# One VectorE-summed mean-square product in place of eight, in a hybrid decoder step on one Trainium2 core

## The reference, cut to what matters

```
def rmsnorm(x, w):
    x32 = x.astype(jnp.float32)
    y = x32 * lax.rsqrt(jnp.mean(x32 * x32, axis=-1, keepdims=True) + RMS_EPS)
    return (y * w.astype(jnp.float32)).astype(x.dtype)
...
    def sub_in(t, i):
        return rmsnorm(t, norm_pre[i]) * (1.0 + m_scale[:, i, None]) + m_shift[:, i, None]

    def sub_out(t, y, i, res):
        return t + res * m_gate[:, i, None] * rmsnorm(y, norm_post[i])

    x = sub_out(x, swiglu(sub_in(x, 0), ffn_up[0], ffn_down[0]), 0, FFN_RES)
    h = sub_in(x, 1)
...
    x = sub_out(x, merged, 1, 1.0)
    x = sub_out(x, swiglu(sub_in(x, 2), ffn_up[1], ffn_down[1]), 2, FFN_RES)
```

## Time and profile before

| what | us |
|---|---|
| median of 3 runs | 2271.89 |
| lowest, highest | 2267.57, 2273.08 |
| the profiled execution | 2272.06 |
| its span | 2270.3 |
| TensorE busy | 2062.6 (91%) |
| VectorE busy | 1257.5 (55%) |
| ScalarE busy | 954.2 (42%) |
| mean granted clock of TensorE | 0.921 of full |

### The profile page before, as it was taken

One profiled execution on the slowest core, in us unless ns is written; L12 is line 12 of the kernel. 1 busy time (PEld: TensorE's weight loads), 2 busy tenths in 40 slices (PEclk: granted clock), 3 DMA queues, 4 the chain that ended last, 5 costly groups with the idle time before them and its releaser, 6 DMA issues.

```text
span 2270.3 us, 44806 instructions
## 1 busy us (share of the span) xinstructions
PE 2062.6 (91%) x19104; PEld 1854.5 (82%) x19104; DVE 1257.5 (55%) x2161; ACT 954.2 (42%) x1872; POOL 4.8 (0%) x30
## 2 busy tenths in 40 slices
PE   5999889889989997899989997989898999879997
PEld 4898868788878876788979996888897878669997
DVE  3554445655446554577556644455653665548863
ACT  4333454444466312433454444434444752153343
POOL 0000000000000000000000000000000000000000
PEclk8999989999999876899999998888999988689998
DMA  7787655556555524588646654443544454158763
GB/s 239 224 232 203 176 149 147 151 149 174 134 149 147 150 74 116 140 244 247 192 124 179 184 171 128 120 117 117 138 108 131 112 125 113 43 134 224 230 193 96
DMA packets 579796, 353.33 MB, mean 156 GB/s; under 512 B 43988, under 2 KB 539638, under 8 KB 578046
## 3 DMA queue, kind: packets, MB, share of 16 engines
q1 hardware_dynamic: 489344, 302.23, 46.9%
q10 hardware_dynamic: 90254, 48.25, 8.7%
HBM read 332.27 MB, written 18.50 MB: 154 GB/s over the span
## 4 chain that ended last, share of the span: by engine, by line
PE 74%; DVE 9%; DMA 6%; ACT 5%; ACTq 4%; issue 3%; SPq 0%; DVEq 0%
PE bank L863 71%; DMA ring<-in_w_ada 3%; DVE ring_r L731 2%; DVE far L1888 1%; ACT w_hi_r L723 1%; DVE big L1888 1%; PE bank L657 1%; PE bank L644 1%; ACTq L1873 1%; DMA ring<-in_ffn_up 1%; ACTq L625 1%; ACTq L570 1%; DVE big L1891 1%; DVE far L1891 1%; PE bank L652 0%
## 5 line engine op out<-in xcount | busy, mean ns | idle before, releaser
L863 PE MATMUL bank<-big_r,w_hi_r 128*128 128x264 f32 x4160 | 1084.5, 295 | 67.8 <-DVE h_r L1888 42.2
L863 PE MATMUL bank<-big_r,ring_r 128*128 128x264 f32 (+1 forms) x3456 | 1001.2, 290 | 0.0
L863 PEld LDWEIGHTS bank<-big_r,w_hi_r 128*128 128x128 f32 x4160 | 757.1, 193 | 141.8 <-issue 94.4
L863 PE MATMUL bank<-h_r,w_hi_r 128*128 128x264 f32 x2752 | 805.0, 293 | 0.0
L731 DVE TENSOR_TENSOR ring_r<-ring,w_hi_r 128x1024 fp32r<-128x1024 f32 (+2 forms) x440 | 524.3, 1196 | 479.6 <-ACT w_hi_r L723 476.0
L863 PEld LDWEIGHTS bank<-big_r,ring_r 128*128 128x128 f32 (+1 forms) x3456 | 671.0, 194 | 1.0
L723 ACT CAST w_hi_r<-ring 128x1024 fp32r<-128x1024 f32 (+2 forms) x440 | 452.2, 1028 | 507.6 <-PE bank L863 293.5
L863 PEld LDWEIGHTS bank<-h_r,w_hi_r 128*128 128x128 f32 x2752 | 539.0, 196 | 1.1
L863 PE MATMUL bank<-big,far 64*64 64x64 f32 (+2 forms) x1440 | 161.6, 268 | 0.0
L863 PEld LDWEIGHTS bank<-big,far 64*64 64x64 f32 (+1 forms) x1440 | 125.6, 144 | 8.1 <-issue 7.5
L863 PE MATMUL bank<-ring,c 128*32 128x256 f32 x1152 | 98.0, 420 | 36.7 <-DMA ring<-in_w_ada 33.4
(11 more groups left out here) (287 smaller groups left out, 1936.8 us busy)
## 6 DMA issues: line engine op xcount, KB each, us to landing
ring<-in_ffn_up SPq DMA_DIRECT2D x176, 512.0 KB, 4.5
ring<-in_w_in SPq DMA_DIRECT2D x148, 512.0 KB, 3.9
ring<-in_w_ada SPq DMA_DIRECT2D x144, 512.0 KB, 4.2
ring<-in_ffn_down SPq DMA_DIRECT2D x64, 512.0 KB, 3.7
far<-in_state_gdn_ssm ACTq DMA_DIRECT2D x28, 512.0 KB, 5.8
ring<-in_ffn_down SPq DMA_DIRECT2D x32, 384.0 KB, 3.2
ring<-in_w_out SPq DMA_DIRECT2D x16, 512.0 KB, 3.9
out_sample_gdn_ssm<-far ACTq DMA_DIRECT2D x16, 512.0 KB, 4.5
```

What stands on the lines that cost most here:

```text
L863: return pe.matmul(out, lhsT, rhs, start=start, stop=stop)
```

## The change

The squares of tiles 1 to 7 are added to tile 0 on VectorE (`add_square`), in place, and TensorE multiplies `mean_all` with this one tile (`mean_of`). In the output stages the add of tile o - 2 stands behind the last `low` of tile o; those of tiles 6 and 7 stand directly ahead of `sub_out`, behind all the other work that VectorE has there. Each add waits for its square and for VectorE's own chain. The means over x keep their eight products. To have a semaphore for the sum (`sq_sum`), `masks_in` is given up, and its two DMAs count on `g2_in`.

```diff
@@ -386,7 +386,7 @@
-        masks_in = signal("masks_in", 16)
+        sq_sum = signal("sq_sum")
@@ -936,6 +936,13 @@
+                    def mean_of(sums):
+
+                        pe.wait_ge(sq_sum.sem, sq_sum.next(pe))
+                        mm(banks[7][:, 0:T], mean_all[:, :], sums[:, 0, :]).then_inc(ss_done.sem, ss_done.one())
+                        for k in range(NT):
+                            sq_ready.next(pe)
+
@@ -972,7 +979,7 @@
                         if l == 0:
                             pe.wait_ge(ada_taken.sem, ada_taken.nth((ADA_FFN, ADA_MIX + ADA_FFN)[i_ffn]))
-                        mean_square()
+                        mean_of(h)
@@ -1191,7 +1198,7 @@
-                                pe.wait_ge(g2_in.sem, g2_in.next(pe))
+                                pe.wait_ge(g2_in.sem, g2_in.nth(3 + l))
@@ -1357,7 +1364,7 @@
-                    mean_square(buf=sq_out)
+                    mean_of(sq_out)
                     mean_square()
                     ffn(1)
@@ -1492,8 +1499,8 @@
-                        act.dma_start(masks[64:128, :, :], masks[0:64, :, :]).then_inc(masks_in.sem, masks_in.one())
-                        act.dma_start(level[64:128, :, :], level[0:64, :, :]).then_inc(masks_in.sem, masks_in.one())
+                        act.dma_start(masks[64:128, :, :], masks[0:64, :, :]).then_inc(g2_in.sem, g2_in.one())
+                        act.dma_start(level[64:128, :, :], level[0:64, :, :]).then_inc(g2_in.sem, g2_in.one())
@@ -1937,6 +1944,18 @@
+                    def add_square(s, o):
+
+                        sums = sq_out if s == 1 else h
+                        if o:
+                            dve.wait_ge(sq_ready.sem, sq_ready.at(NT * (2 * s + 1) + o + 1))
+                            dve.wait_ge(dve_chain.sem, dve_chain.all())
+                            i = tt(sums[:, 0, :], sums[:, 0, :], sums[:, o, :], ALU.add)
+                            if o == NT - 1:
+                                i.then_inc(sq_sum.sem, sq_sum.one())
+                            else:
+                                i.then_inc(dve_chain.sem, dve_chain.one())
+
@@ -1983,12 +2002,16 @@
                         for n in range(3 * NT):
                             ahead(dve, low, (l, f"down{i_ffn}", n))
+                            if n % 3 == 2 and n // 3 >= 2:
+                                add_square(2 * i_ffn, n // 3 - 2)
                         if i_ffn == 0 and l == 0:
                             conditioning(ADA_FIRST + 2, ADA_FFN)
                             scales(1)
                         if i_ffn == 1 and l + 1 < DEPTH:
                             take_parameters()
                             next_layer()
+                        for o in (NT - 2, NT - 1):
+                            add_square(2 * i_ffn, o)
                         sub_out(2 * i_ffn)
@@ -2001,7 +2024,7 @@
-                        dve.wait_ge(masks_in.sem, masks_in.next(dve, 2))
+                        dve.wait_ge(g2_in.sem, g2_in.nth(2))
@@ -2388,10 +2411,14 @@
                     for o in range(NT):
                         ahead(dve, low, (l, "out", o))
+                        if o >= 2:
+                            add_square(1, o - 2)
                     for e in range(2):
                         i = tt(vnx[:, e, :, :], bm(vnrow[:, e, :], NS), bc(delta[:, :], P))
                     i.then_inc(vnx_ready.sem, vnx_ready.one())
                     dve.wait_ge(vnx_ready.sem, vnx_ready.all())
+                    for o in (NT - 2, NT - 1):
+                        add_square(1, o)
                     sub_out(1)
```

## The result

| | before | changed |
|---|---|---|
| median us (7 runs each) | 2271.89 | 2282.54 |
| lowest, highest | 2267.57, 2274.2 | 2275.77, 2287.59 |
| the profiled execution, its span | 2272.06, 2270.3 | 2282.54, 2280.8 |
| mean granted clock | 0.921 | 0.914 |

The ratio is 1.0052 (95% interval 1.0035 to 1.0070): slower, by more than the 0.3% that a measurement tells from no change, and half a us above the range forecast. In two later sets on other occasions, each beside its own runs of the kernel before, the same kernel came out at 1.0033 (1.0008 to 1.0058) and 1.0032 (1.0008 to 1.0056).

A forecast was written before the change was run, and what follows sets the result against it. It took TensorE (busy 91%) to bound the long weight-product stretches. Tail 1.66, x-pass clock 1.6 and half-clock lone products 1.5 summed to +4.8 us, giving 2276.6 us (0.2% more), range 2269.5 to 2282.

The forecast's parts named there:

- end 6: Layer 1's second FFN output: nothing left on VectorE, only the last square counts, so the root starts 1.94 us sooner.
- The tail at full clock: Last weight product to ScalarE's root over y, six sublayer ends: adds queue behind VectorE's work; +1.66 us in sum.
- the lone products at half clock: The one y product left at each of five ends takes 0.54 us more at half clock; +1.5 us.
- end 4: Layer 1's first FFN output: root sooner by 0.52 us, taken as -0.45 as the y step may have awaited ScalarE's copy.
- Ends 2 and 5: Mixing outputs of both layers: two `vnx` multiplications hold VectorE ahead of the adds; root +0.93 us later at each.
- End 3: Layer 0's second FFN output: the next layer's parameters hold VectorE ahead of the adds; root +2.13 us later.
- end 1: Layer 0's first FFN output: VectorE's split and conditioning precede the last adds; root +0.06 us later.
- The clock in the x passes: Five mean-square passes over x, each following an end: low clock at their start, back at full within some; +1.6 us.
- the clock decides: Rival: x passes and lone products run at low clock, +9.9 us to 2281.8; needs over 5.1 us of clock; chance 0.25.
- The adds are free and the saving comes everywhere: Rival: VectorE as free at each end as at end 6, gaining 11.6 us, to 2260.3; chance 0.05.
- The adds delay the splits: Rival, output stages: adds ahead of late-DMA splits cost 0.43 us each, 12.9 for all 30, to 2289.5; chance 0.04.

The follow-up runs named there:

- e2: Changed kernel's 42 VectorE adds written to a spare tile, with all eight TensorE products kept; ratio 1.0007 against the kernel before.
- e5: The changed kernel run again without edit, in a later set; ratio 1.0033 against the kernel before.
- e12: The changed kernel run a third time, in another set; ratio 1.0032 against the kernel before.
- e3: Changed kernel plus products of constants on TensorE ahead of the lone y product; ratio 1.0015 against the kernel before.
- e4: Changed kernel with VectorE's side work (conditioning, vnx, parameters) moved behind sub_out; ratio 1.0005 against the kernel before.
- e9: Changed kernel plus products of constants ahead of and behind the lone product and behind the x pass; ratio 1.0004 against the kernel before.
- e10: Changed kernel with only VectorE's last weight split of each end moved behind the last add; ratio 0.9963 against the kernel before.
- e7: Changed kernel with last adds ahead of the last split, side work late, and constant products behind y product and x pass; ratio 0.9935 against before.
- e11: Changed kernel with the last split behind the adds, plus constant products behind the y product and x pass; ratio 0.9946 against the kernel before.
- e6: Changed kernel with the last three adds ahead of the last weight split and side work behind sub_out; ratio 0.9981 against the kernel before.
- e8: Kernel before (eight products, no adds) plus products of constants behind its y and x means; ratio 0.9974 against the kernel before.

## Why the prediction was wrong

It forecast +0.2%, 4.8 us, and a range to 2282; measured was +0.5%, 10.7 us between the medians and 2282.54. The direction and the mechanism were right: the saving appears at end 6 alone, and elsewhere VectorE's order eats it. The signs it named are there: at end 2 the add of tile 6 starts at 917.89 as the `vnx` multiplications end, and TensorE has no new idle time in the FFN output stages (e2). Two steps failed. In the sum it was the tail, end 4 above all. In the range it was the spread, which stood in the low end alone. Of the 5.9 us missing, 1.7 are in the tails and 0.5 in the x lengths; 3.6 lie outside the ends, in two stretches whose lengths vary by 3.6 and 5.9 us over the 14 profiles; whether that is all spread is open.

- *The tail at full clock*, forecast +1.66 us, with +1.5 for the lone products at half clock: 3.2. Measured +4.8, +4.9 and +5.0 in three profiles. This is the term of the sum that failed, and within it **end 4**, which I put at -0.45: it was +0.60, +0.76 and +1.24. I took the starts of before as given, and so put a later DMA at nothing. But the split ahead of the adds hangs on a DMA that ScalarE waited 2.70 us for before and 3.61 in the changed kernel. Eight products had hidden that DMA's lateness; with the adds behind the split every tenth of a us of it is on the path. I had named the late DMA only as a danger within the output stage. The profiles show it from two sides. In all six kernels that keep the split first with one product behind it (the changed one, e5, e12, e3, e4, e9) the root of end 4 comes 4.53 or 4.54 us after the start of that cast, or 5.06 and 5.07 where the product is at half clock (e12, e5), while the tail ranges from 3.54 to 5.12. In e3 the cast is as early as in the kernel before, and end 4 is -0.34, near the forecast. In e10, with the split behind the adds, end 4 takes 2.34 us though its DMA is late (3.40 us of waiting). Why the DMA is later stays open: the wait is 2.70 to 2.73 us in the three kernels with eight products, 3.23 to 3.95 in eight of the eleven profiles with one product, and 2.60 to 2.72 in the other three (e3, e7, e11). (At e9's 3.95 the profile names TensorE, not the DMA, as what ended the wait.)
- *Ends 2 and 5*: +0.93 each forecast, 1.47 with the half clock; measured +1.49 at both, and 0.96 in e3, with the full clock. Right.
- *End 3*: +2.13, or 2.67 at half clock; measured +2.91. A chain of two adds takes 0.54 us from one to the next and not 0.46, and the first waits longer: some 0.2 us at each end, which also makes end 1 +0.22 in place of +0.06.
- *End 6*: -1.94 forecast, -1.89 measured.
- *The clock in the x passes*: +1.6 forecast, 30.93 us busy against about 30.4; measured +2.1, +2.3 and +3.1. Right in size, a little low. The lone product was at half clock at ends 2, 3 and 5 of the first profile, so 1.6 us against the 1.5 assumed. One reading behind the term was wrong: at full clock it is not ScalarE's squares that set the pace of an x pass. At end 3 of before each square waits 0.26 or 0.27 us for VectorE's add into `xT`, and VectorE gives one tile every 0.69 us. The Trainium skill's warning ("TensorE: Matmul & The Clock Gate", section "HAM oscillation — how this bites in real kernels") is borne out in part: all five x passes of the changed kernel ran at an average clock of 0.59 to 0.62, and their lengths sum to 44.7 to 45.7 us against the floor of 39.9 (e9). But in the kernel before, two of the five ran at full clock.
- *The rival "the clock decides"*, +9.9, gave the better number, but by luck. It asked for more than 5.1 us of clock; the x lengths and the lone products together gave 3.7, 4.5 and 4.7 us in the three profiles. And with the clock held up wholly (e9) the tails still stand 3.2 us above those of before. *"The adds are free and the saving comes everywhere"* fails for this change and holds for the tails of e6, where nothing stands ahead of the adds (11.1 us saved, 11.6 priced). *"The adds delay the splits"* falls with e2 and the equal output stages.
- *The range.* I allowed 1.3 us for the spread of the rest, from three runs within 5.5 us, and only at the low end; the high end is the first rival's sum with no spread at all. The kernel before, with 35 runs in one set, covered 2261 to 2287. The two later ratios, 1.0033 and 1.0032, would put the changed kernel at 2279.4 and 2279.2, inside the range.

## What to carry to other kernels

When work is handed from a queue with slack to another engine, look at what stands ahead of it there at that very moment, and put the piece on which the path hangs first: one weight split moved at each end turned +0.3% into -0.4%. Count in what stands ahead of it every wait for a DMA, as lateness that eight products had hidden comes out in full. Where TensorE has nothing to do for some us between dense stretches, products of constants into an unused bank can pay: in the kernel before 0.3% (e8, interval 0.01 to 0.5%). And a range needs the spread of the runs at both of its ends.

## What was not expected of the hardware

With the tail filled and only the gap of 2.8 us behind the product left empty, the x passes still ran partly at half clock (e3, x lengths 44.1 us against 39.9). With 2.4 us of constants in that gap (0.54 us left) the clock stayed at 1.00 from root to root at all five ends of e7, e8 and e9. In e11 it averaged 0.79 at end 3, where TensorE had idled 2.37 us ahead of the product, and yet the length was 7.99. And two adds of 128x264, each behind two semaphore waits and dependent on the other, start 0.54 us apart, of which 0.44 is the add.
